# The second recurrence's chunk matrices held as dense 64x64 blocks on quarters of the array

## The reference

```python
def step(S, inp):                       # S: (heads, 64, 64)
    r_t, w_t, k_t, v_t, a_t, b_t = inp
    Sa = einsum('bhij,bhj->bhi', S, a_t)
    S = S * w_t + Sa[..., None] * b_t + v_t[..., None] * k_t
    return S, einsum('bhij,bhj->bhi', S, r_t)   # over 512 tokens
```

## Time and profile before

| what | value |
|---|---|
| median of three runs | 3662.53 us |
| the profiled execution's own time | 3656.49 us |
| its span | 3654.7 us |
| mean granted TensorE clock | 0.974 |
| TensorE busy | 3479.7 us |
| VectorE busy | 1820.7 us |
| ScalarE busy | 1243.3 us |
| window of inverse, scan and outputs | 367.56 to 590.53 us |

### The profile page before, as it was taken

The page is one execution under the profiler, slowest core; times in us unless marked ns, Lnnn a source line. Parts: engine busy times, 40 slices in busy tenths (PEclk is TensorE's granted clock), DMA queues, the critical chain, the costliest instruction groups (busy, mean ns, idle before and its releaser), DMA issues.

```text
span 3654.7 us, 47335 instructions
## 1 busy us (share of the span) xinstructions
PE 3479.7 (95%) x16942; PEld 2829.5 (77%) x16942; DVE 1820.7 (50%) x3463; ACT 1243.3 (34%) x1637; POOL 802.9 (22%) x334
## 2 busy tenths in 40 slices
PE   8998998799988989998999999999999899999998
PEld 6665996588766778887887888788888688888886
DVE  3564442433115552333113499998888254444443
ACT  2223211333235543334224333354544233323332
POOL 6430001244432323333444344400000000000000
PEclk9988999899999999999999999999999999999999
DMA  3110000122221112222223244455555655555542
GB/s 128 56 37 0 1 2 22 54 98 98 88 97 63 57 63 75 75 75 69 91 94 100 81 145 146 130 180 173 181 172 185 224 198 190 198 203 201 196 143 75
DMA packets 145931, 407.80 MB, mean 112 GB/s; under 512 B 11176, under 2 KB 43944, under 8 KB 143536
## 3 DMA queue, kind: packets, MB, share of 16 engines
q1 hardware_dynamic: 73472, 265.85, 22.7%
q10 hardware_dynamic: 72368, 140.68, 10.7%
HBM read 337.28 MB, written 69.21 MB: 111 GB/s over the span
## 4 chain that ended last, share of the span: by engine, by line
PE 83%; DVE 13%; ACT 2%; issue 1%; ACTq 1%; DMA 1%; DVEq 0%
PE bank L325 22%; PE bank L327 22%; PE bank L326 22%; PE bank L857 2%; PE bank L855 1%; PE bank L354 1%; DVE arena L1664 1%; PE bank L556 1%; ACT arena L898 1%; PE bank L791 1%; PE bank L542 1%; PE bank L465 1%; DVE arena L1793 1%; PE bank L427 1%; PE bank L546 1%
## 5 line engine op out<-in xcount | busy, mean ns | idle before, releaser
L325 PE MATMUL bank<-xs,ring_hi 128*128 128x512 f32 x2488 | 996.8, 401 | 63.7 <-DVE xs L1372 31.1
L327 PE MATMUL bank<-xs,ring_lo 128*128 128x512 f32 x2488 | 975.6, 392 | 0.0
L326 PE MATMUL bank<-xs,ring_hi 128*128 128x512 f32 x2488 | 975.0, 392 | 0.0
L1343 POOL TENSOR_TENSOR ring_lo<-ring,ring_hi 128x1024 fp32r<-128x1024 f32 x262 | 650.7, 2486 | 1062.6 <-ACT ring_hi L898 1062.6
L898 ACT ACTIVATE arena<-bank 128x512 f32<-128x512 f32 (+5 forms) x612 | 408.3, 698 | 1143.6 <-PE bank L327 745.1
L898 ACT ACTIVATE ring_hi<-ring 128x1024 fp32r<-128x1024 f32 x469 | 495.5, 1059 | 504.4 <-DMA ring<-weights 241.3
L325 PEld LDWEIGHTS bank<-xs,ring_hi 128*128 128x128 f32 x2488 | 471.1, 189 | 174.1 <-issue 38.2
L327 PEld LDWEIGHTS bank<-xs,ring_lo 128*128 128x128 f32 x2488 | 470.7, 189 | 101.9
L326 PEld LDWEIGHTS bank<-xs,ring_hi 128*128 128x128 f32 x2488 | 471.9, 190 | 98.6 <-issue 4.6
L1806 DVE TENSOR_TENSOR ring_lo<-ring,ring_hi 128x1024 fp32r<-128x1024 f32 x206 | 252.3, 1225 | 404.4 <-ACT ring_hi L898 404.4
L325 PE MATMUL bank<-gw,ring_hi 128*128 128x512 f32 x1024 | 398.5, 389 | 0.7 <-ACT arena L898 0.7
(11 more groups left out here) (271 smaller groups left out, 4049.1 us busy)
## 6 DMA issues: line engine op xcount, KB each, us to landing
ring<-weights SPq DMA_DIRECT2D x503, 512.0 KB, 3.3
hidden<-arena ACTq DMA_DIRECT2D x128, 256.0 KB, 3.9
gates<-arena ACTq DMA_DIRECT2D x16, 2048.0 KB, 6.6
arena<-hidden ACTq DMA_DIRECT2D x16, 2048.0 KB, 10.7
arena<-gates ACTq DMA_DIRECT2D x16, 2048.0 KB, 17.2
xres<-x_t ACTq DMA_DIRECT2D x4, 512.0 KB, 5.8
out_t<-arena SPq DMA_DIRECT2D x1, 2048.0 KB, 7.1
arena<-ret_decay ACTq DMA_DIRECT2D x1, 1024.0 KB, 5.6
```

What stands on the lines that cost most here:

```text
L325: pe.matmul(out_, wh, x[0], start=start, stop=False, skip_group_check=True)
L326: pe.matmul(out_, wh, x[1], start=False, stop=False, skip_group_check=True)
L327: return pe.matmul(out_, wl, x[0], start=False, stop=stop, skip_group_check=True)
L1343: pool.tensor_tensor(ring_lo[:, r, :], ring[:, r, :], ring_hi[:, r, :].bitcast(F32), ALU.subtract).then_inc(lo_done, 1)
```

## The change

The matrices are held densely. A tile of 128x512 now holds both heads of a pair: partitions 64p to 64p+63 hold the chunks of parity p = c mod 2, and the free dimension holds 2 heads x 4 chunks x 64 columns. `quad(ap, p, j, g)` names one 64x64 block, and `chunks` multiplies the 16 blocks of a pair, each a 64x64x64 product whose operands and result lie on the same half of the partitions. HS[s] now belongs to a pair, and two pairs (s = 0, 1) are worked on in each of two rounds r, where there were four rounds of one pair with two heads. Each level gets two dummy products. In the scan the old state is added in PSUM by a product with the identity (`state_part`), the products with the keys are issued a chunk ahead, the scores of a head are one group of 16 products with one mask instruction, and the result alternates between banks 7 and 4. The outputs are formed for two pairs at a time from 64x64x64 products, in two halves. VectorE changes the constants `strict` and `strict_T` in the setup, by six small copies. The diff, cut to its core (indentation reduced by eight):

```diff
@@ buffers @@
-HS = [[40, 41, 42, 43, 44, 45, 46, 47], [48, 49, 70, 71, 72, 73, 74, 50]]
+HS = [[42, 41, 40, 43, 44, 45, 46, 47], [70, 49, 48, 71, 72, 73, 74, 50]]
-MS = [(40, 41), (42, 43), (44, 45), (46, 47), (48, 49), (70, 71), (72, 73), (16, 17)]
+MS = [40, 41, 42, 43, 44, 45, 46, 47]
-RW_PE, RW_ACT, RW_DVE = 28, 16, 12
+RW_PE, RW_ACT, RW_DVE = 28, 18, 12
@@ TensorE @@
+    def quad(ap, p, j, g):
+        return ap[p * HD:(p + 1) * HD, (TT * j + g) * C:(TT * j + g + 1) * C]
+    def chunks(dst, l, r):
+        for j in range(2):
+            for c in range(NCH):
+                g, p = c // 2, c % 2
+                mm = pe.matmul(quad(dst, p, j, g), quad(l, p, j, g), quad(r, p, j, g), start=True, stop=True,
+                               skip_group_check=True)
+        return mm
-    for m in range(NPAIR):
-        for e in range(2):
-...
+    for r in range(2):
+        for s in range(2):
+            m, b0 = 2 * r + s, 3 * s
+            if r == 0:
+                pe.wait_ge(rw_act, 36)
+            else:
+                pe.wait_ge(rw_act, 36 + RW_ACT - 1 + s)
+                pe.wait_ge(rw_dve, 8 + RW_DVE)
+            for c in range(NCH):
+                g, p = c // 2, c % 2
+                cols = slice(c * C, (c + 1) * C)
+                for k, (l, r_) in enumerate(((TB, TA), (TA, TB))):
+                    for e in range(2):
+                        rows = slice(e * HD, (e + 1) * HD)
+                        pe.matmul(quad(bank[b0 + e], p, k, g), tile(l + m)[rows, cols], tile(r_ + m)[rows, cols],
+                                  start=True, stop=True, skip_group_check=True)
+            for c in range(NCH):
+                g, p = c // 2, c % 2
+                cols = slice(c * C, (c + 1) * C)
+                for e in range(2):
+                    rows = slice(e * HD, (e + 1) * HD)
+                    mm = pe.matmul(quad(bank[(b0 + 2, 7 - s)[e]], p, e, g), tile(TK + m)[rows, cols],
+                                   tile(TA + m)[rows, cols], start=True, stop=True, skip_group_check=True)
+            mm.then_inc(rw_pe, 1)
+        for lev in range(5):
+            for s in range(2):
+                hs, b0 = HS[s], 3 * s
+                a, b = (0, 1) if lev % 2 == 0 else (1, 0)
+                pe.wait_ge(rw_dve, 8 + RW_DVE * r + 2 * lev + s + 1)
+                if s == 0:
+                    keep_clock(7, 1)
+                mm = chunks(bank[b0], tile(hs[2 + a]), tile(hs[a]))
+                if lev < 4:
+                    mm = chunks(bank[b0 + 1], tile(hs[a]), tile(hs[2 + a]))
+                mm.then_inc(rw_pe, 1)
+            for s in range(2):
+                hs, b0 = HS[s], 3 * s
+                a, b = (0, 1) if lev % 2 == 0 else (1, 0)
+                if s == 0:
+                    keep_clock(7, 1)
+                pe.wait_ge(rw_act, 36 + RW_ACT * r + 2 * lev + s + 1)
+                chunks(bank[b0 + 2], tile(hs[b]), tile(hs[4 + a])).then_inc(rw_pe, 1)
+        for s in range(2):
+            m, hs, b0 = 2 * r + s, HS[s], 3 * s
+            pe.wait_ge(rw_dve, 8 + RW_DVE * r + 10 + s + 1)
+            for e in range(2):
+                for c in range(NCH):
+                    g, p = c // 2, c % 2
+                    mm = pe.matmul(quad(bank[b0], p, e, g), quad(tile(hs[6]), p, e, g),
+                                   v4(tile(MV + m))[p * HD:(p + 1) * HD, g, e * HD:(e + 1) * HD],
+                                   start=True, stop=True, skip_group_check=True)
+            mm.then_inc(rw_pe, 1)
+            for g in range(TT):
+                for e in range(2):
+                    cols_h = slice(e * HD, (e + 1) * HD)
+                    for p in range(2):
+                        mm = pe.matmul(bank[(b0 + 1, 7 - s)[p]][cols_h, g * C:(g + 1) * C],
+                                       v4(tile(MA + m))[p * HD:(p + 1) * HD, g, cols_h], quad(tile(hs[5]), p, e, g),
+                                       start=True, stop=True, skip_group_check=True)
+            mm.then_inc(rw_pe, 1)
+        for s in range(2):
+            hs, b0 = HS[s], 3 * s
+            pe.wait_ge(rw_act, 36 + RW_ACT * r + 10 + 3 * s + 1)
+            chunks(bank[b0 + 2], tile(hs[5]), tile(hs[7])).then_inc(rw_pe, 1)
+    base_pe, base_act, base_dve = 36 + RW_PE * 2, 36 + RW_ACT * 2, 8 + RW_DVE * 2
-...
-    def head_scores(h, k):
+    SBANK = (7, 4)
+    def head_scores(h):
         ...
+        for k in range(2):
+            for c in range(NCH):
+                g, p = c // 2, c % 2
+                cols = slice(c * C, (c + 1) * C)
+                mm = pe.matmul(quad(bank[h % 2], p, k, g), tile((TK, TB)[k] + m)[rows, cols], tile(TR + m)[rows, cols],
+                               start=True, stop=True, skip_group_check=True)
+    def state_part(c, part):
+        g, p = c // 2, c % 2
+        trow = slice(p * HD, (p + 1) * HD)
+        for h in range(8):
+            m, e = h // 2, h % 2
+            rows = slice(e * HD, (e + 1) * HD)
+            if part == "keys":
+                l, r_ = v4(tile(MK + m))[trow, g, rows], v4(tile(MV + m))[trow, g, rows]
+            elif part == "state":
+                l, r_ = cc("ident")[rows, rows], shv[rows, c, m * HD:(m + 1) * HD]
+            else:
+                l, r_ = v4(tile(MB + m))[trow, g, rows], tile(UU + g)[trow, h * HD:(h + 1) * HD]
+            mm = pe.matmul(bank[SBANK[c % 2]][rows, m * HD:(m + 1) * HD], l, r_,
+                           start=(part == "keys" and h < 2), stop=(part == "removal"), skip_group_check=True)
+        return mm
-    keep_clock(7, 4)
+    keep_clock(3, 4)
     ...
+    state_part(0, "keys")
     for c in range(NCH):
-        keep_clock(4, 1)
+        keep_clock(3, 1)
         if c > 0:
-            pe.wait_ge(rw_dve, base_dve + 4 * c - 1)
+            pe.wait_ge(rw_dve, base_dve + 3 * c)
            ...
+            if c < NCH - 1:
+                st.go(state_part(c, "state"))
-        head_scores(c, 0)
+        head_scores(c)
+        if c + 1 < NCH - 1:
+            state_part(c + 1, "keys")
         if c < NCH - 1:
-            ...
+            pe.wait_ge(rw_dve, base_dve + 3 * c + 1)
+            st.sync()
+            state_part(c, "removal").then_inc(rw_pe, 1)
-        head_scores(c, 1)
+    bp, bd, ba = base_pe + 22, base_dve + 23, base_act
-...
-    keep_clock(4, 2)
+    keep_clock(3, 2)
     ...
+    def y_local(m, p, g, e, part, start):
+        h, rows, trow = 2 * m + e, slice(e * HD, (e + 1) * HD), slice(p * HD, (p + 1) * HD)
+        v = v4(tile(MV + m))[trow, g, rows] if part == 0 else tile(UU + g)[trow, h * HD:(h + 1) * HD]
+        pe.matmul(bank[4 + m % 2][rows, (2 * g + p) * C:(2 * g + p + 1) * C], v, quad(tile(MS[h]), p, part, g),
+                  start=start, stop=True, skip_group_check=True)
+    def y_state(m, e, c):
+        rows, cols = slice(e * HD, (e + 1) * HD), slice(c * C, (c + 1) * C)
+        return pe.matmul(bank[4 + m % 2][rows, cols], shv[rows, c, m * HD:(m + 1) * HD], tile(TR + m)[rows, cols],
+                         start=False, stop=True, skip_group_check=True)
+    for r in range(2):
+        if r:
+            pe.wait_ge(rw_act, ba + 2)
+        for half in range(2):
+            keep_clock(6, 2)
+            if half:
+                st.sync()
+            for g in range(TT):
+                for part in range(2):
+                    for e in range(2):
+                        for s in range(2):
+                            y_local(2 * r + s, (half + s) % 2, g, e, part, half == 0 and g == 0 and part == 0)
+            for c in range(1, NCH):
+                for s in range(2):
+                    mm = y_state(2 * r + s, (half + s) % 2, c)
+            if half == 0:
+                st.go(mm)
         mm.then_inc(rw_pe, 1)
@@ ScalarE @@
+    for r in range(2):
+        pb = 36 + RW_PE * r
+        for lev in range(5):
+            for s in range(2):
+                act.wait_ge(rw_pe, pb + 2 + 4 * lev + s + 1)
+                A(tile(HS[s][1 if lev % 2 == 0 else 0]), bank[3 * s][:, :], ACT.Copy).then_inc(rw_act, 1)
+        for s in range(2):
+            act.wait_ge(rw_pe, pb + 22 + 2 * s + 1)
+            A(tile(HS[s][7]), bank[3 * s][:, :], ACT.Copy).then_inc(rw_act, 1)
+            act.wait_ge(rw_pe, pb + 22 + 2 * s + 2)
+            for p in range(2):
+                A(tile(WT + 2 * r + s).rearrange("p (g q t) -> p g q t", q=2, t=C)[:, :, p, :],
+                  bank[(3 * s + 1, 7 - s)[p]][:, 0:256].rearrange("p (g t) -> p g t", t=C), ACT.Copy).then_inc(rw_act, 1)
+        for s in range(2):
+            m = 2 * r + s
+            act.wait_ge(rw_pe, pb + 26 + s + 1)
+            A(arena[:, U0:U0 + 4, m * P:(m + 1) * P].rearrange("p g (e i) -> p g e i", e=2),
+              bank[3 * s + 2][:, :].rearrange("p (e g i) -> p g e i", e=2, g=4), ACT.Copy).then_inc(rw_act, 1)
-...
-        act.wait_ge(rw_pe, bp + 2 * m + 2)
+        act.wait_ge(rw_pe, bp + m // 2 + 1)
@@ VectorE @@
+    for a, b in (("strict", "incl_T"), ("strict_T", "ident")):
```

(111 more changed lines are left out.)

101 lines of the change are left out of this document (9 added, 92 removed).

## The result

The changed kernel takes 3557.66 us (median of four runs, 3555.84 to 3565.97) against 3657.5 (3649.61 to 3670.58) for the kernel before beside it: a ratio of 0.9723, 95% interval 0.9696 to 0.9749, some 100 us less. The profiled execution took 3555.84, its span is 3554.0, and the mean clock 0.974 as before.

What follows compares the result with a forecast made beforehand. TensorE's pitch was taken to bound inverse, scan and outputs. 66.1 + 5.4 + 17.2 - 1.0 = 87.7 us off the profiled 3656.5 gave 3568.8, or 3575 against the median; range 3548 to 3640.

Steps and rivals of the forecast that it cites:

- Inverse: Inverse stage: 2560 records for two rounds, priced at 0.029 us, plus dummies and waits; 88.6 us against 154.7, -66.1.
- Scan: Scan stage: a chunk's period of 3.6 us instead of 4.34; 29.6 us against 35.0, -5.4.
- Outputs: Outputs stage: four halves of 92 records, 2.74 us each, plus dummies and waits; 16.1 us against 33.3, -17.2.
- bound (a): Scores, `WT` products and outputs: if 880 records on four quarters overlapped by four, 12.8 us less; 0.029 was taken.
- Setup: Setup: six small VectorE copies on the path add 1.0 us, bounds 0 and 3.
- Rival one: Levels, ends and state products: two diagonal quarters of one bank take turns, 0.058 a record, 62.2 us more, 3637; chance 0.11.
- Rival two: New stages: instruction issue becomes the bound, 0.067 us a record, 3688, deciding above 0.060; chance 0.05.
- Rival three: New stages: small products lower the clock; in part 5 to 25 us (chance 0.07), in full 87 us more, 3662 (0.03).

Runs made afterwards that it cites:

- e5: The changed kernel with score products ordered by chunk parity and local output products by pair, so two quarters alternate instead of four: 3562.46 us, ratio 0.9737.
- after: The changed kernel itself, against the kernel before: 3557.66 us, ratio 0.9723.
- e3: The changed kernel without the setup's six copies, the dense masks built in the table of constants: 3556.57 us, ratio 0.9711 to the kernel before.
- e4: The kernel before with six copies of the same size added in the setup, written to scratch that nothing reads: 3667.35 us, ratio 1.0024.
- e2: The changed kernel with `chunks` reordered, all even chunks then all odd, eight records in a row on one quarter: 3569.47 us, ratio 0.9756 to the kernel before.
- e8: The changed kernel with `chunks` reordered by parity for both heads, sixteen records in a row on one quarter: 3639.94 us, one run.
- e1: The changed kernel without the 20 dummy products of the inverse's levels: 3551.92 us, ratio 0.9715 to the kernel before.

## Why the prediction was right

The mechanism held: TensorE's pitch bounds the three stages, and dense blocks on two quarters cut them about as priced. The forecast of 3575 was 17 us above the time. In the profiled execution (3568.8 forecast, 3555.84 measured) the miss of 13 is -11.9 in the three stages, +4.8 in the setup, -6.3 in the attention and +0.5 behind. That the setup's excess and the attention's nearly cancel is chance as far as the runs show. By its steps:

- **Inverse, -66.1 forecast, -71.2 measured.** `chunks` at 0.029 and the level of 6.8 us (6.75) were right. The scores were mis-sized: I priced 192 records a round at 0.029 = 5.6 us, and they run at 0.015, 2.8 us less. In the first round 0.9 of that went into the wait for the masks (1.48 us, where I had 0.6), in the second TensorE stood still for 1.59 us inside the scores, with no releaser in the profile. The products with a at the ends, 128 records in all, run at the same pitch, 1.9 us less.
- **Scan, -5.4 and -8.3.** The chunk takes 3.2, not 3.6: from the first `WT` product to the dummy 2.60 us for 96 records instead of 2.85, and from there to the next `WT` product 0.59 instead of 0.75. Six periods of 0.4 are 2.4 of the 2.9. The scan changed in more than its blocks (the state added in PSUM, the key products a chunk ahead, one mask instruction), and no run takes these apart.
- **Outputs, -17.2 and -21.1.** 256 records over four quarters, again 0.015 instead of 0.029: 3.7 of the 3.9.
- So the term that was off is the overlap by four, bound (a)'s lower end, "12.8 us less", which I took at nothing because no row had it. e5 shows it from the other side: without it, +1.3 and +2.9.
- **Setup, +1.0 forecast with bounds 0 and 3; L409 is 4.8 later in two pairs of kernels.** I took 0.5 for a copy stretched beside GpSimd; two were stretched by 1.6 and 2.2. The bound was too narrow. Whether the whole time of the changed kernel carries it stays open (after against e3); the kernel before does get slower by the copies (e4).
- **Rival one, the quarters take turns,** is refuted: each 32 records in a row go to two quarters of one bank, at 0.029. A rule of the Trainium skill (TensorEngine Tiling (Array Packing), Restrictions and Gotchas) says that different row tiles cannot access the same PSUM bank simultaneously; here two row tiles with different columns and different output partitions do so at 0.029, where e5's scores, on two row tiles with a bank each, have 0.026, and the measurement decides. What taking turns would cost is the gap between a quarter's own records, 0.058; e2 and e8 with their part of it have 0.038 and 0.049.
- **Rival two, the issue as bound,** is refuted: 64 records on end at 0.015, where it asked for at least 0.060, and the pitch does not grow over 128. The 62 ns for each MATMUL that the Trainium skill's page TensorE: Matmul & The Clock Gate, section Back-to-back issue gap, gives for hardware decode off do not hold in this trace, with its 15 ns; whether decode was on no run shows.
- **Rival three, the clock,** did not come in the changed kernel, 1.00 in all three windows, and not even without the levels' dummies (e1). But it can happen: e8 ran 85 us at 0.50 with TensorE fully busy. The size of the products, by which I had argued, does not decide it alone: it is the same in after, e2 and e8. Inside the inverse the clock fell only with long runs on one quarter, so the change's loop order, with c alternating in parity, probably kept it; the prediction did not see this. It is not shown as a rule, since e8's second round kept 1.00 in the same order.
- **Small slips in the working:** L556's pitch is 0.115, not 0.116, and the terms of a round of the inverse add up to 44.2, not 44.3. Neither moves the forecast.

## What to carry to other kernels

Price small products by how many quarters of the array they walk over in turn, not by their number: the same 64x64 record cost 0.015, 0.029, 0.038 or 0.049 us here by the order of the loops alone. When block-diagonal 128x128 tiles become dense 64x64 blocks, let successive products walk over all four quarters where the data allows it, and never stay long on one; with two, it mattered little whether they differed in one half (0.026) or in both (0.029). Then see whether what feeds them keeps up (here waits took back about a third of what the scores gained). And once a stage is dense by itself, take its dummy products out and look at the granted clock: 8.9 us lay there.

## What the runs showed that I had not expected

- Four quarters overlap by four: 64 float32 records of 64x64 start in 0.98 us (477.21 to 478.19), 0.015 apart, where one quarter's own are 0.058 apart. All runs on four quarters here use two banks; four in one bank were not tried.
- Eight records in a row on one quarter have a mean pitch of 0.038, not 0.058. As the starts read, records to a free quarter begin before the queue for a busy one is through.
- TensorE can be busy for 85.30 of 85.30 us and be granted half its clock in all of it (e8, with sixteen records in a row on one quarter), and in the same kernel and order be busy for 55.53 of 55.53 us at full clock. With eight in a row it was 3.4 us in the whole inverse (e2).
- A VectorE copy of 64x64, 0.19 us long, took 1.81 and 2.39 us while a GpSimd instruction of 128x1024 ran, each ending within 0.1 us of GpSimd's. A cause is not shown by an experiment, only that the times go together, in after and in e4's copies. In e3, without the copies, the 8x512 subtraction that follows them in after at 0.68 us takes 2.26 instead, so part of the stretch seems to move to whatever comes next.
